# Output side of a hybrid decoder layer: projections run column block by column block, weights streamed three times, norms moved under the next block

## The chip, the cores and the metric

The kernel runs on one core of a Trainium2 chip. The metric is the device time of one execution in microseconds (us), lower is better. Engines are named as in the profile: PE is TensorE, DVE VectorE, ACT ScalarE, POOL GpSimd, SP SyncE, which here issues most transfers.

## What is computed

One layer of a decoder on 1024 prompt tokens and 64 new tokens (8 sequences of 8), all in float32. Only its second half matters here:

```
a_proj = a_out @ p['w_attn_out']          # (tokens, 512) @ (512, 1024)
b_proj = y @ p['w_ssd_out']
mixed = (gate_a * a_proj + gate_b * b_proj) @ p['w_out']   # (1024, 1024)
x = x + rmsnorm(mixed, p['post_mix_norm'])
h2 = rmsnorm(x, p['pre_ffn_norm'])
gu = h2 @ p['w_up']                       # (1024, 5632)
f = (silu(gu[..., :D_FF]) * gu[..., D_FF:]) @ p['w_down']
x = x + rmsnorm(f, p['post_ffn_norm'])
```

Ahead of it stand the input projection, a Mamba branch, the prompt attention and the attention of the new tokens over their caches (the sample stage).

## The kernel before

Tensors lie transposed: 128 channels on the partitions, T = 1088 tokens along the free axis, KD = 8 tiles of channels for a width of 1024. The tokens are cut into three column blocks c = 0, 1, 2 (`TH`: 368, 368, 352 columns), one PSUM bank each. A float32 product is made from three matmuls: every operand is split in a high part (`hH`, `aH`, `wH`) and a low part (`hL`, `aL`, `wL`), and `into` (lines 1637 to 1647) issues high by high, high by low, low by high for each tile of the inner axis (four tiles in the attention projection, eight in the output projection).

Weights come in chunks. SP loads a chunk to one of two raw buffers (`load`, line 434); POOL splits it in one of three slots (`split`: a cast, L646, and a subtraction, L648); PE multiplies with it for all three column blocks. SP may load chunk n when chunk n-2 is split, POOL may split chunk n when PE has finished with chunk n-3. Before, the attention projection has 8 chunks of 128x512 and the output projection 8 of 128x1024 elements; each serves one tile m of output channels and three blocks.

The order of each engine's work is written out by hand, and engines meet at semaphores. The stretch around the change, in its old order:

- PE: for m, for c: attention projection (bank c, freed by DVE). DVE multiplies the gates in (L1540, L1542 with the PSUM input, L1545) into `acc8`, whose start values (the Mamba branch, `ba_scr`) SP loads tile by tile together with the gates (L558, L563, L564).
- When all 24 tiles are mixed, ACT writes `hH` (L1108) and DVE `hL` (L1549); PE starts the output projection when the eight tiles of block 0 are there. ACT moves its results to `m2` (L798).
- Then the two norms, for all blocks together. ACT squares tiles of 1088 columns (L808), PE adds them up with a matrix of ones (`sums`, L1656), ACT takes the root (L816), DVE the reciprocal (L1556, L1186). DVE scales and adds to `x1` (L1559, L1562), and after the second norm writes scaled tiles and low halves (L1188, L1180).
- PE starts the feed-forward product (`up`) on block c when that block's halves are there. It has 11 groups of 4 up chunks and 2 down chunks.

SP's transfer of x (`xt_scr` to `x1`, L571) stands behind the last gates, ahead of the first chunk of `w_out`.

Of the kernel before, what the change touches and what calls it, by code (L numbers as in the profile page):

```python
# [22 lines left out]
ACT = mybir.ActivationFunctionType  # L23
# [6 lines left out]
P = 128  # L30
# [48 lines left out]
U_NORME = U_OUT + KD + 1  # L79
U_NORMF = U_NORME + 1  # L80
U_FF = U_NORMF
# [8 lines left out]
C_OUT = C_PROJ + KD  # L90
C_FF = C_OUT + KD
# [3 lines left out]
def trunk(nc, x_prompt, x_sample, cache0, cache1, cache2, state_conv, state_ssm, pre_mix_norm, w_in,  # L95
# [5 lines left out]
    with ctx:  # L101
# [56 lines left out]
        base[0] += 3 * T * 4  # L158
# [24 lines left out]
        rs = at("rs", [P, T], off=T0 + 2 * T * 4)  # L183

# [67 lines left out]
        G, A = ps[0:3], ps[3:8]  # L252
        RING = [G[0], G[1], G[2], A[0]]
# [22 lines left out]
        def gap(c, rows=P):  # L276
            return G[c][0:rows, 0:TH[c][1] - TH[c][0]]

# [28 lines left out]
        ba_in, xt_in, x1_done, facc_zero = sem("ba_in"), sem("xt_in"), sem("x1_done"), sem("facc_zero")  # L307
# [33 lines left out]
        mix_in = [sem(f"mix_in{m}") for m in range(KD)]  # L341
# [58 lines left out]
        def stages():  # L400
# [3 lines left out]
            yield C_OUT, 1, lambda i: [(wou[:, :, m * P:(m + 1) * P], KD, P) for m in range(KD)]  # L404
# [8 lines left out]
        def _(sp):  # L413
# [94 lines left out]
            for stage, (first, rounds, chunks) in enumerate(stages()):  # L508
                per = len(chunks(0))
                if stage == 2:  # L510
# [28 lines left out]
                    load_k(1)  # L539

# [7 lines left out]
                    for m in range(2):  # L548
                        load(C_PROJ + m, wao[:, :, m * P:(m + 1) * P], NJ, P, C_PROJ + m)
                    sp.wait_ge(spv_ready, DB - 1)  # L550
                    load_v(DB - 1)

                    for q in gate_out:
                        sp.wait_ge(q, 32 * KD + 1)
                    sp.wait_ge(g_ready[2], U_PROJ - 1)
                    for m in range(2):
                        for k in range(2):
                            sp.dma_start(gates[k][:, m, :], gate_scr[k, m]).then_inc(mix_in[m], 16)  # L558
                    sp.wait_ge(spv_ready, DB)
                    for m in range(KD):  # L560
                        if m >= 2:
                            for k in range(2):
                                sp.dma_start(gates[k][:, m, :], gate_scr[k, m]).then_inc(mix_in[m], 16)  # L563
                        sp.dma_start(acc8[:, m, :], ba_scr[:, m, :]).then_inc(mix_in[m], 16)  # L564
                        if m + 2 < KD:
                            load(C_PROJ + m + 2, wao[:, :, (m + 2) * P:(m + 3) * P], NJ, P, C_PROJ + m + 2)
                    continue
                if stage == 3:
                    sp.wait_ge(aL_ready, 2 * NJ + 1)

                    sp.dma_start(x1[:, :, :], xt_scr).then_inc(xt_in, 16)  # L571
# [39 lines left out]
        def _(pool):  # L611
# [158 lines left out]
            for m in range(KD):  # L770
                split(C_PROJ + m, U_PROJ + max(m - 2, -1), NJ, P, C_PROJ + m)
            for m in range(KD):
                split(C_OUT + m, U_OUT + m - 2, KD, P, C_OUT + m)
            for t in range(3):
                split(C_FF + t, U_OUT + 6 + t, KD, P, C_FF + t)
            pool.wait_ge(x1_done, 2 * KD)
# [16 lines left out]
        def _(act):  # L793
# [311 lines left out]
            act.wait_ge(mix_step, 9 * KD)  # L1105
            for c in range(3):
                for f in range(KD):
                    act.copy(cols(hH[:, f, :], c), cols(acc8[:, f, :], c)).then_inc(hH_ready, 1)  # L1108
            for m in range(KD):
                for c in range(3):  # L1110
                    evac(c, U_OUT + m + 1, [(cols(m2[:, m, :], c), gap(c))])
            for c in range(3):
                act.wait_ge(g_free[c], U_OUT + KD)
            squares(m2, KD, 8, 7)
            roots(KD, U_NORME)
            squares(x1, KD, 16, 14, lambda f: act.wait_ge(x1_done, 2 * f + 2))
            roots(KD, U_NORMF)
            halves(3 * KD)

            act.wait_ge(hL_ready, 72)  # L1120

            def hidden(k, u):
# [972 lines left out]
```

## Time and profile before

| | us |
|---|---|
| median of 3 runs | 3412.22 (3406.45 to 3413.03) |
| the profiled execution | 3417.95 |
| its span, first to last instruction | 3415.0 |
| PE busy, share of the span | 91% |
| mean granted clock of PE | 0.933 |

The profiled execution is 5.7 us longer than the median, and 2.95 us of it lie outside its span. Times inside it are given from the start of the span.

### The profile page before, as it was taken

What the parts mean: (1) busy time and instruction counts of PE and PEld (TensorE: products, weight loads), DVE (VectorE), ACT (ScalarE), POOL (GpSimd) and SP (SyncE); (2) the same over time, 40 slices, a digit from 0 to 9 for tenths busy, and PEclk for the clock granted to TensorE, in tenths of its full rate; (3) what the DMA queues carried; (4) which work ended last, traced back from release to release, by engine and by line L of the source; (5) the groups of instructions that cost most, each with busy time, mean ns of one, the idle gap of its engine ahead of it and who ended that gap; (6) DMA issues with size and microseconds to landing.
All of it is one profiled execution on the core that took longest, in us unless ns stands there. A gap on an engine that the chain in (4) does not pass through costs nothing.

```text
span 3415.0 us, 47987 instructions
## 1 busy us (share of the span) xinstructions
PE 3107.6 (91%) x18365; PEld 2886.6 (85%) x18365; DVE 1394.7 (41%) x2781; ACT 736.8 (22%) x1632; POOL 771.1 (23%) x539
## 2 busy tenths in 40 slices
PE   5699999999999999999999927998887999999998
PEld 3698898899789889989899925778867999999997
DVE  4566648556654755222122251113334223322225
ACT  3232132313312320232232211110122000000003
POOL 1222222222222122212121000001312322322222
PEclk8799999999999999999999967777999999999999
DMA  4233333424333342112212054445300111111112
GB/s 140 84 125 116 104 130 85 158 90 124 115 102 120 103 145 91 46 41 56 61 35 67 17 135 125 139 143 197 114 28 25 44 44 44 49 42 48 44 44 67
DMA packets 324378, 297.59 MB, mean 87 GB/s; under 512 B 23232, under 2 KB 291056, under 8 KB 322840
## 3 DMA queue, kind: packets, MB, share of 16 engines
q1 hardware_dynamic: 240502, 239.40, 22.8%
q10 hardware_dynamic: 83674, 55.24, 5.5%
q8 instruction: 158, 2.59, 0.3%
q14 instruction: 44, 0.36, 0.0%
HBM read 247.00 MB, written 101.34 MB: 102 GB/s over the span
## 4 chain that ended last, share of the span: by engine, by line
PE 85%; DVE 9%; DMA 2%; issue 2%; ACT 1%; SPq 1%; POOL 0%; DVEq 0%; ACTq 0%; POOLq 0%
PE ps L1644 21%; PE ps L1646 21%; PE ps L1645 21%; PE ps L1969 3%; DVE ssde L1304 2%; PE ps L1746 2%; PE ps L1849 2%; PE ps L1870 2%; PE ps L1919 1%; PE ps L1753 1%; PE ps L1752 1%; PE ps L1861 1%; PE ps L1798 1%; PE ps L1795 1%; PE ps L1656 1%
## 5 line engine op out<-in xcount | busy, mean ns | idle before, releaser
L1644 PE MATMUL ps<-hH,wH 128*128 128x368 f32 (+2 forms) x3480 | 1165.5, 335 | 55.2 <-issue 44.7
L1646 PE MATMUL ps<-hH,wL 128*128 128x368 f32 (+2 forms) x3480 | 1146.0, 329 | 0.0
L1645 PE MATMUL ps<-hL,wH 128*128 128x368 f32 (+2 forms) x3480 | 1145.5, 329 | 0.0
L1644 PEld LDWEIGHTS ps<-hH,wH 128*128 128x128 f32 (+1 forms) x3480 | 657.8, 189 | 101.2 <-issue 84.0
L1645 PEld LDWEIGHTS ps<-hL,wH 128*128 128x128 f32 (+1 forms) x3480 | 658.2, 189 | 1.9
L1646 PEld LDWEIGHTS ps<-hH,wL 128*128 128x128 f32 (+1 forms) x3480 | 657.2, 189 | 2.1
L646 POOL CAST wH<-wraw 128x1024 fp32r<-128x1024 f32 (+2 forms) x191 | 195.5, 1024 | 1787.5 <-PE ps L1646 1306.1
L648 POOL TENSOR_TENSOR wL<-wraw,wH 128x1024 fp32r<-128x1024 f32 (+2 forms) x191 | 451.4, 2363 | 15.3
L1575 DVE TENSOR_TENSOR sq<-sq,ps 128x368 f32<-128x368 f32 (+1 forms) x66 | 35.1, 532 | 434.0 <-PE ps L1646 434.0
L1446 DVE COPY atp<-ps 128x256 f32<-128x256 f32 (+1 forms) x96 | 52.5, 547 | 328.1 <-PE ps L1861 328.1
L1644 PE MATMUL ps<-uH,wH 128*128 128x368 f32 (+1 forms) x528 | 176.0, 333 | 0.7 <-DVE m L1584 0.7
L1645 PE MATMUL ps<-uL,wH 128*128 128x368 f32 (+1 forms) x528 | 173.6, 329 | 0.0
L1646 PE MATMUL ps<-uH,wL 128*128 128x368 f32 (+1 forms) x528 | 173.4, 328 | 0.0
L1584 DVE TENSOR_TENSOR m<-m,ps 128x368 f32<-128x368 f32 (+1 forms) x240 | 123.3, 530 | 81.1 <-PE ps L1646 79.8
L1644 PE MATMUL ps<-yH,wH 128*128 128x368 f32 (+1 forms) x384 | 129.5, 337 | 22.3 <-DVE gpart L1421 17.0
L1304 DVE SCALAR_TENSOR_TENSOR ssde<-ssde,tokg,ssdbcb 128x128 f32<-128x128 f32 (+1 forms) x288 | 132.1, 526 | 11.0 <-ACT ssdbcb L900 11.0
L798 ACT COPY qkv<-ps 128x368 f32<-128x368 f32 (+1 forms) x108 | 59.1, 547 | 341.6 <-PE ps L1646 288.7
L1969 PE MATMUL ps<-smpt,smvraw 128*128 128x16 f32 x576 | 115.9, 351 | 17.2 <-DMA smvn<-out_dram 10.4
L1969 PEld LDWEIGHTS ps<-smpt,smvraw 128*128 128x128 f32 x576 | 112.7, 301 | 19.4 <-issue 18.5
L1295 DVE SCALAR_TENSOR_TENSOR ssdc<-ssdc,ccg,ssdc 128x1112 f32<-128x1112 f32 x72 | 109.7, 1524 | 46.8 <-ACT ssdc L938 45.1
L1645 PE MATMUL ps<-yL,wH 128*128 128x368 f32 (+1 forms) x384 | 127.3, 332 | 0.0
L1646 PE MATMUL ps<-yH,wL 128*128 128x368 f32 (+1 forms) x384 | 127.1, 331 | 0.0
(295 smaller groups left out, 3976.7 us busy)
## 6 DMA issues: line engine op xcount, KB each, us to landing
wraw<-in_w_in_dram SPq DMA_DIRECT2D x92, 512.0 KB, 3.9
wraw<-in_w_up_dram SPq DMA_DIRECT2D x44, 512.0 KB, 3.8
ssdcr<-cum_scr ACTq DMA_DIRECT2D x32, 512.0 KB, 4.8
out_dram<-in_cache_kv_w_dram SPq DMA_DIRECT2D x16, 960.0 KB, 5.5
wraw<-in_w_down_dram SPq DMA_DIRECT2D x22, 512.0 KB, 3.7
smkraw<-in_cache_kv_w_dram SPq DMA_DIRECT2D x40, 256.0 KB, 6.6
smvraw<-in_cache_kv_w_dram SPq DMA_DIRECT2D x40, 256.0 KB
ssds<-in_state_ssm_dram ACTq DMA_DIRECT2D x16, 512.0 KB, 5.4
```

Of the source, the lines that this page charges most:

```text
L646: pool.tensor_copy(wH[b][:, 0:k], a[:, 0:k]).then_inc(w_hi, 1)
L648: pool.tensor_tensor(wL[b][:, 0:k], a[:, 0:k], wH[b][:, 0:k].bitcast(F32), ALU.subtract).then_inc(w_split, 1)
L1295: dve.scalar_tensor_tensor(out=cacc[:, 0:CWID - 3], in0=cr[:, i:i + CWID - 3], scalar=ccg[:, m, 24 + i:25 + i], in1=cacc[:, 0:CWID - 3], o ...
L1304: ins = dve.scalar_tensor_tensor(out=dec[c % 2][0:n, h, 0:n], in0=dec[c % 2][0:n, h, 0:n], scalar=tokg[0:n, c, 1, h:h + 1], in1=bcb[0:n, P ...
L1584: dve.tensor_tensor(cols(m2[:, m, :], c), cols(m2[:, m, :], c), gff(c, m + 1), ALU.add).then_inc(g_free[c], 1)
L1644: pe.matmul(dst, hi, cols(mH[:, k, :], c), start=k == 0, stop=False)
L1645: pe.matmul(dst, hi, cols(mL[:, k, :], c), start=False, stop=False)
L1646: last = pe.matmul(dst, lo, cols(mH[:, k, :], c), start=False, stop=k == kt - 1)
L1746: pe.matmul(A[2][0:n, h * 64:h * 64 + 64], dec[c % 2][0:n, h, 0:n], xtok[0:n, h * 64:h * 64 + 64], start=True, stop=True)
L1849: mm = pe.matmul(A[1 + s][:, 0:w], tokens(qT, gr, i)[rows], keys(kT, gr, i)[rows], start=True, stop=True)
L1870: mm = pe.matmul(A[4][:, 64 * s:64 * s + 64], pt[i % 2][:, s * len(bl) + b, :], vtok[gr][:, t, 64 * s:64 * s + 64], start=b == 0, stop=b = ...
L1969: pe.matmul(A[4][:, 16 * j:16 * j + 16], vraw[:, t, j * P:(j + 1) * P], pts[:, t, 16 * j:16 * j + 16], start=t == 0, stop=False)
```

## The change

- The attention projection goes block by block: for c, for m. Its chunks are now 128x1024 and hold two m; the four of them are loaded and split three times (12 instead of 8 small ones). The same holds for the output projection: 8 chunks, three times (24).
- PE writes to a ring of six banks (`RING6`) instead of one bank a block.
- DVE mixes a block at a time. The halves of block 0 are made before blocks 1 and 2 are mixed.
- ACT squares each tile of 368 columns as it evicts it, and DVE adds the squares up (`out_square`, `x1_square`), where PE did. PE issues one sum a norm and block (`e_sums`, `f_sums`). The norms of block c stand among the products of block c + 1 on all three engines; those of block 2 stand under the first feed-forward products of blocks 0 and 1, which are reordered for it.
- SP loads all gates in the sample stage, and ba_scr in three transfers, one a block.

```diff
 (SP)
+                    for m in range(KD):
+                        for k in range(2):
+                            sp.dma_start(gates[k][:, m, :], gate_scr[k, m]).then_inc(gates_in, 16)
                     with sp.Fori(0, DB - 2) as b:
...
+                    for c in range(3):
+                        sp.dma_start(cols3(acc8, c), cols3(ba_scr, c)).then_inc(ba_in[c], 16)
+                    for n in range(2, 3 * (KD // 2)):
+                        load_proj(n)
+                        if n == 5:
+                            sp.wait_ge(aL_ready, 2 * NJ + 1)
+                            sp.dma_start(x1[:, :, :], xt_scr).then_inc(xt_in, 16)
+                    for n in range(3 * KD):
+                        m = n % KD
+                        load(C_OUT + n, wou[:, :, m * P:(m + 1) * P], KD, P, C_OUT + n)
 (POOL)
+            for n in range(C_PROJ, C_FF + 3):
+                c, u = last_use(n - SPL)
+                pool.wait_ge(g_ready[c], u)
+                kt, w = (NJ, 2 * P) if n < C_OUT else (KD, P)
+                split(n, 0, kt, w, n, guard=False)
 (ACT)
+            def out_evict(c, m):
...
+                act.copy(cols(m2[:, m, :], c), src)
...
+                    if n >= 3:
+                        act.wait_ge(essum_step, (KD - 1) * c + max(m - 2, 0))
+                act.activation(dst[:, 0:w], src, ACT.Square).then_inc(g_free[c], 1)
 (DVE)
+            mix(0)
+            mixed_low(0)
+            mix(1)
+            mix(2)
+            mixed_low(1)
+            mixed_low(2)
+            for m in range(1, KD):
+                out_square(0, m)
             dve.wait_ge(xt_in, 16)
...
+            for c in range(2):
+                factor_e(c)
+                x1_rows(c, 0, 4)
+                out_square(c + 1, 1)
+                x1_rows(c, 4, 8)
+                out_square(c + 1, 2)
+                out_square(c + 1, 3)
+                factor_f(c)
+                h2_rows(c, 0, 3)
...
+            factor_e(2)
+            x1_rows(2, 0, 8)
+            factor_f(2)
+            h2_rows(2, 0, 8)
 (PE)
+            for c in range(3):
+                for m in range(KD):
+                    out_product(c, m)
+                    if c and m == 0:
+                        e_sums(c - 1)
+                    if c and m == 4:
+                        f_sums(c - 1)
...
+            pe.wait_ge(hL_ready, 48 + 2 * KD)
...
+            up_part(0, 0)
+            e_sums(2)
+            up_part(0, 1)
...
+            up_part(1, 0)
+            up_part(1, 1)
...
+            up_part(2, 0)
+            f_sums(2)
+            up_part(2, 1)
+            pe.wait_ge(hL_ready, 48 + 3 * KD)
+            for i in range(3):
+                up_part(i, 2)
```

On DVE, the norms began before as follows (after the last low half of the mixing; `rs` holds the factors of all blocks, `m_165` is m2, `x_166` x1):

```order
L1556 RECIPROCAL rs<-rs 128x368 x2
L1556 RECIPROCAL rs<-rs 128x352
L1559 SCALAR_TENSOR_TENSOR m_165<-m_165,nrm,rs 128x1088
L1562 TENSOR_TENSOR x_166<-x_166,m_165 128x1088
L1559 SCALAR_TENSOR_TENSOR m_165<-m_165,nrm,rs 128x1088
```

And this is DVE's queue now where the second norm of block 1 begins (`mid_96` collects block 2's squares of the output, `mid_92` and `mid_93` hold one tile's; `mid_97` is the factor, `mid_98` and `mid_99` scaled tiles):

```order
L1643 TENSOR_TENSOR mid_96<-mid_96,mid_93 128x352
L1683 RECIPROCAL mid_97<-mid_97 128x368
L1697 SCALAR_TENSOR_TENSOR mid_98<-x_175,nrm,mid_97 128x368
L1697 SCALAR_TENSOR_TENSOR mid_99<-x_175,nrm,mid_97 128x368
L1689 TENSOR_TENSOR hL<-mid_98,hH 128x368
L1697 SCALAR_TENSOR_TENSOR mid_98<-x_175,nrm,mid_97 128x368
L1689 TENSOR_TENSOR hL<-mid_99,hH 128x368
L1643 TENSOR_TENSOR mid_96<-mid_96,mid_92 128x352
```

The norm of one block and the square additions of the next stand in one queue, and every tile is a block wide instead of 1088 columns. The additions of 352 columns are block 2's, the rest is block 1's.

On SP, before, the transfers behind the last V rows began with the gates of tiles 0 and 1; this piece is the middle of them:

```order
L558 DMA gate_a<-gate_scr 128x1088
L558 DMA gate_b<-gate_scr 128x1088
L564 DMA acc_73<-ba_scr 128x1088
L434 DMA wraw_52<-in_w_attn_out_dram 128x4x128
L564 DMA acc_73<-ba_scr 128x1088
L434 DMA wraw_51<-in_w_attn_out_dram 128x4x128
L563 DMA gate_a<-gate_scr 128x1088
L563 DMA gate_b<-gate_scr 128x1088
```

Now:

```order
L570 DMA acc_73<-ba_scr 128x8x368 x2
L570 DMA acc_73<-ba_scr 128x8x352
L440 DMA wraw_52<-in_w_attn_out_dram 128x4x256
L440 DMA wraw_51<-in_w_attn_out_dram 128x4x256
L440 DMA wraw_52<-in_w_attn_out_dram 128x4x256
L440 DMA wraw_51<-in_w_attn_out_dram 128x4x256
L575 DMA x_175<-xt_scr 128x8704
L440 DMA wraw_52<-in_w_attn_out_dram 128x4x256
```

The gates are gone from here, all of ba_scr stands ahead of the third chunk, and the transfer of x ahead of the seventh.

## Rows read from the trace of the kernel before

**Rows 1.** The page: span; busy us, share and instructions of each engine.

```profile
span 3415.0 us, 47987 instructions
PE 3107.6 (91%) x18365; PEld 2886.6 (85%) x18365; DVE 1394.7 (41%) x2781; ACT 736.8 (22%) x1632; POOL 771.1 (23%) x539
```

**Rows 2.** Busy time by stage: stretch, its length, engines, PE's granted clock, DMA share, GB/s.

```profile
2359.00:2410.00 51.00, 49.60 (x288) 49.30 (x288) 42.57 (x71) 0.00 (x0) 15.88 (x14) 0.97 0.96 357
2410.00:2421.00 11.00, 0.21 (x1) 0.24 (x2) 10.34 (x12) 9.06 (x23) 7.86 (x5) 0.66 0.47 142
2421.00:2517.40 96.40, 96.31 (x576) 96.02 (x576) 6.79 (x16) 11.23 (x26) 24.01 (x14) 0.99 0.13 39
2517.40:2599.00 81.60, 49.42 (x170) 34.42 (x171) 57.91 (x70) 36.75 (x52) 10.74 (x3) 0.81 0.02 7
2599.00:2634.60 35.60, 35.60 (x218) 35.60 (x217) 5.68 (x7) 2.94 (x5) 10.31 (x6) 1.00 0.15 45
```

**Rows 3.** POOL in order of time, feed-forward part: start us, us.

```profile
2610.90 1.04 POOL L646 CAST wH<-wraw 128x1024 fp32r<-128x1024 f32 x1 [8.36 <-PE ps L1646]
2612.02 2.40 POOL L648 TENSOR_TENSOR wL<-wraw,wH 128x1024 fp32r<-128x1024 f32 x1
...
2622.76 1.04 POOL L646 CAST wH<-wraw 128x1024 fp32r<-128x1024 f32 x1 [8.34 <-PE ps L1646]
```

**Rows 4.** POOL in order of time, in the feed-forward loop.

```profile
2771.44 1.04 POOL L646 CAST wH<-wraw 128x1024 fp32r<-128x1024 f32 x1 [26.32 <-PE ps L1646]
...
2774.90 1.04 POOL L646 CAST wH<-wraw 128x1024 fp32r<-128x1024 f32 x1
...
2780.12 1.04 POOL L646 CAST wH<-wraw 128x1024 fp32r<-128x1024 f32 x1 [1.73 <-DMA wraw<-in_w_up_dram]
```

**Rows 5.** DMA issues, 2380 to 2420: count, KB each, us to landing.

```profile
x<-xt_scr SPq DMA_DIRECT2D x1, 4352.0 KB, 19.9
wraw<-in_w_out_dram SPq DMA_DIRECT2D x5, 512.0 KB, 3.6
```

**Rows 6.** POOL in order of time, first chunks of w_out.

```profile
2410.20 1.33 POOL L646 CAST wH<-wraw 128x1024 fp32r<-128x1024 f32 x1
2411.61 2.51 POOL L648 TENSOR_TENSOR wL<-wraw,wH 128x1024 fp32r<-128x1024 f32 x1
2414.09 1.32 POOL L646 CAST wH<-wraw 128x1024 fp32r<-128x1024 f32 x1
```

**Rows 7.** DVE in order of time, the same stretch.

```profile
2407.95 2.68 DVE L1540 TENSOR_TENSOR acc<-acc,gate_b 128x352 f32<-128x352 f32 x1
2410.55 0.51 DVE L1542 TENSOR_TENSOR gate_a<-gate_a,ps 128x352 f32<-128x352 f32 x1
...
2412.47 2.05 DVE L1549 TENSOR_TENSOR hL<-acc,hH 128x368 fp32r<-128x368 f32 x1 [0.56 <-ACT hH L1108]
```

**Rows 8.** DVE in order of time, one mixing and the next.

```profile
2376.50 0.53 DVE L1540 TENSOR_TENSOR acc<-acc,gate_b 128x368 f32<-128x368 f32 x1
...
2378.03 0.52 DVE L1540 TENSOR_TENSOR acc<-acc,gate_b 128x352 f32<-128x352 f32 x1
```

**Rows 9.** DVE in order of time, the second norm.

```profile
2564.05 2.45 DVE L1186 RECIPROCAL rs<-rs 128x368 f32<-128x368 f32 x1 [2.79 <-ACT rs L816]
...
2567.71 0.54 DVE L1180 TENSOR_TENSOR hL<-sq,hH 128x368 fp32r<-128x368 f32 x1
2568.17 0.59 DVE L1188 SCALAR_TENSOR_TENSOR sq<-x,nrm,rs 128x368 f32<-128x368 f32 x1
2568.68 0.53 DVE L1180 TENSOR_TENSOR hL<-sq,hH 128x368 fp32r<-128x368 f32 x1
```

**Rows 10.** DVE's first mixing and what it waited for.

```profile
2361.86 0.54 DVE L1540 TENSOR_TENSOR acc<-acc,gate_b 128x368 f32<-128x368 f32 x1 [2.80 <-DMA acc<-ba_scr]
```

**Rows 11.** PE in order of time, sample stage: transposes of the third batch's K rows.

```profile
2121.82 0.90 PE L1919 MATMUL ps<-ident,smkraw 128*128 128x128 f32 x3
```

**Rows 12.** ACT in order of time: roots of the first norm.

```profile
2531.47 1.28 ACT L816 ACT_TABLE_LOAD   x1
2532.79 1.76 ACT L816 ACTIVATE rs<-ps,eps 128x368 f32<-128x368 f32 x3
```

More of the change, by code:

```diff
@@ L183, in trunk @@
         rs = at("rs", [P, T], off=T0 + 2 * T * 4)
+        sE1, sqE0, sqE1, sqF0, sqF1, sE0, sF, hv0, hv1 = [at(f"mid{i}", [P, TH[0][1]], off=T0 + i * TH[0][1] * 4) for i in range(9)]
+        sE, sqE, sqF, hvb = [sE0, sE1], [sqE0, sqE1], [sqF0, sqF1], [hv0, hv1]
         xs = at("xs", [P, XT, T], off=X1)
@@ L1109, in _ @@
             for m in range(KD):
[L1110 to L1122, printed above, removed]
+                out_evict(0, m)
@@ new lines, in silu_first @@
+            def silu_first(c):
+                act.wait_ge(g_ready[c], U_FF + 1)
+                act.activation(cols(sq[0], c), gff(c, 1), ACT.Silu).then_inc(g_free[c], 1)
+            root_e(2)
+            act.wait_ge(uL_ready, 1)
+            for f in range(0, 4):
+                x1_square(2, f)
+            silu_first(0)
+            for f in range(4, 8):
+                x1_square(2, f)
+            silu_first(1)
+            root_f(2)
+            for f in range(8):
+                h2_high(2, f)
@@ L1124, in hidden @@
+            silu_first(2)
+            def hidden(k, u, first=False):
                 par = k_par(k)
                 for i in range(2):
-                    for c in range(3):
+                    for c in (() if first and i == 0 else range(3)):
                         act.wait_ge(uL_ready, k * 2 + i + 1)
@@ L1139, in k_par @@
                 return 1 if k_even[0] else 0
[L1141 removed]
+            hidden(0, U_FF, first=True)
             with act.Fori(0, 5) as i:
@@ L1996, in _ @@
-            sums(KD, U_NORME, 8)
-            sums(KD, U_NORMF, 16)
-            def up(n, u, n0, first=False):
+            for c in range(3):
+                pe.wait_ge(g_free[c], U_PROJ)
+            for c in range(3):
+                for m in range(KD):
+                    n, k = c * KD + m, C_PROJ + c * (KD // 2) + m // 2
+                    if m % 2 == 0:
+                        pe.wait_ge(w_split, k + 2)
+                    if n >= 6:
+                        cp, mp = LAST[n - 6]
+                        pe.wait_ge(g_free[cp], U_PROJ + mp + 1)
+                    into(RING6[n % 6][:, 0:TH[c][1] - TH[c][0]], c, k % SPL, NJ, 2 * P, m % 2 * P, P, aH, aL)
@@ new lines, in out_product, with e_sums @@
+            def out_product(c, m):
+                n, k = c * KD + m, C_OUT + c * KD + m
+                pe.wait_ge(w_split, k + 2)
+                if m == 0:
+                    pe.wait_ge(hL_ready, 24 + KD * (c + 1))
+                cp, mp = LAST[n - 6]
+                pe.wait_ge(g_free[cp], (U_OUT if n >= 6 else U_PROJ) + mp + 1)
+                into(RING6[n % 6][:, 0:TH[c][1] - TH[c][0]], c, k % SPL, KD, P, 0, P, hH, hL)
+            def e_sums(c):
+                w = TH[c][1] - TH[c][0]
+                pe.wait_ge(essum_step, (KD - 1) * (c + 1))
+                if c:
+                    pe.wait_ge(rsE_act, c)
+                pe.matmul(A[3][:, 0:w], ones[:, :], sE[c % 2][:, 0:w], start=True, stop=True).then_inc(esum_ready, 1)
@@ new lines, in f_sums @@
+            def f_sums(c):
+                w = TH[c][1] - TH[c][0]
+                pe.wait_ge(fssum_step, (KD - 1) * (c + 1))
+                if c:
+                    pe.wait_ge(rsF_act, c)
+                pe.matmul(A[4][:, 0:w], ones[:, :], sF[:, 0:w], start=True, stop=True).then_inc(fsum_ready, 1)
+            for c in range(3):
+                for m in range(KD):
+                    out_product(c, m)
[3 more added lines that the diff above has]
+                        f_sums(c - 1)
```

238 lines of the change are left out of this document (166 added, 72 removed).

## The prediction

> **What bounds the kernel now.** The page gives the whole: a span of 3415.0 us in a run of 3417.95 us, TensorE busy for 91% of it, no other engine above 41% [rows 1]. Shares do not price this change, so the next view is the busy time by stage: one row each for projection, gap, output projection, norms and the first four chunks of the feed-forward product [rows 2]. I call that stretch, 2359.0 to 2634.6, the middle: 275.6 us. The reader is to see where TensorE is not full: 11 us between projection and output projection (0.21 us busy), and 81.6 us behind the output projection with 170 recorded matmuls.
>
> What must be done there on TensorE is 288 + 576 + 288 = 1152 matmuls. In the feed-forward part four splits of GpSimd in a row, of which two are shown, each released by TensorE's last matmul on an older chunk, follow one another every 11.86 us [rows 3], and a chunk is 3 blocks of 24 matmuls: 0.165 us per matmul, 3.95 us per block. So 1152 matmuls are 190 us, and 86 us of the middle are waits, sums of squares and half clock. That is all the change can win, 2.5%. The half clock is in the windows too: the mean granted clock is 0.97 over the 51 us of the projection, which starts after a wait, and 1.00 in the feed-forward part. If it was at the lower level (1.2 for 2.4 GHz) for 3 us, 1.5 us were lost; I take 1.6 us for each start after a wait of some 10 us.
>
> **What the change removes.** The 11 us go (mixing of all 24 tiles, then their halves), since the halves of block 0 are ready early. Of the norms, blocks 0 and 1 go under products; only block 2 stays in the open, under five of its neighbours' products. If nothing else were late, the middle would be 190 + 4 (six sums) plus what is left open, priced with the rivals.
>
> **What it adds.** 1. Weights. 12 + 24 chunks instead of 8 small + 8: each chunk now feeds 24 matmuls, 3.95 us, not 11.86 us. A split of 1024 columns is 1.04 + 2.40 us and repeats after 3.46 us when GpSimd is alone [rows 3, 4]. A load lands 3.6 us after its issue [rows 5], just about the length of one split, and two raw buffers take turns. GpSimd alone would hold TensorE's pace by 0.5 us a chunk.
>
> 2. The port. GpSimd is not alone. In [rows 6] and [rows 7] both engines are saturated for a moment. A VectorE operation with both inputs in SBUF takes 0.53 us [rows 8], but 2.68 and 2.05 us when it meets GpSimd's subtraction, and GpSimd's cast stretches from 1.04 to 1.33 us. One cycle of cast and subtraction is then 3.89 us and lets through just two such VectorE operations at 0.4 us of work: the split itself holds the other off for 3.1 us. The multiplication that reads PSUM (L1542) keeps its 0.51 us beside GpSimd. A reciprocal (2.4 us, one SBUF input) stands beside a split in no row; the nearest is L1542, also with one SBUF input, so I let the six run free. Held, each waits at most one subtraction more, 6 x 2.2 = 13 us. [...]
>
> Before, the middle had 12 full-size splits, most of them far apart. Now it has 38 of them: 38 x 3.1 = 118 us. VectorE's operations with two SBUF inputs are 48 (mixing), 24 (low halves), 21 + 21 (sums of squares, which TensorE did before), 24 additions, 24 low halves of the second norm: 162 at 0.45 us from start to start, and 48 scalings at 0.51, 97 us [rows 9]. Together 215 us on one lock, against 190 us of TensorE. So I take VectorE with GpSimd as the new bound, and follow their chain.
>
> 3. The start. ba_scr now comes in three transfers of a block, 1472 KB instead of 544 KB for the first. At the 357 GB/s of this stage [rows 2] that is 2.7 us more, so the first mixing starts at 2364.5 instead of 2361.86 [rows 10]. The third weight chunk queues behind all three blocks (12.5 us), so TensorE, done with two chunks at 2368, waits some 9 us. x1 (4352 KB) takes 10 to 20 us in the queue [rows 5] and holds the seventh chunk for some 5 us. Both waits lie ahead of a VectorE that is late anyway.
>
> 4. The gates (16 x 544 KB, 8.9 MB) move into the sample stage, behind the K rows of the second batch. At 357 GB/s they run to about 2113 and the next K rows, queued behind them, land by 2121; the transposes that need them start at 2121.8 [rows 11]. Zero on the path, with 1 us to spare.
>
> **The chain, from the first mixing.**
> - To the first sum e(0), a sum standing behind block 0's seven square additions: VectorE's 24 mixings at 1.53 us [rows 8], 24 halves and 7 additions at 0.45 are 50.7 us; 22 splits (chunks 3 to 24) are 68.2 us; the 24 multiplications that run beside them take off 10.8. 2364.5 + 108.1 = 2472.6.
> - e(0) to f(0): sum 0.6, table 1.28, root 0.6, reciprocal 2.4 [rows 9, 12]; 8 scalings, 8 additions, 7 square additions and one of the next block are 11.3; TensorE makes four products meanwhile, so four splits, 12.4. Together 28.6: 2501.2. TensorE's four products need 15.8, so it waits about 10 us at f(0).
> - f(0) to e(1): 3.6 + 20 operations 9.5 + four splits 12.4 = 25.5: 2526.7.
> - e(1) to f(1): 27.3 (no table): 2554.0. f(1) to the last halves of block 1: 3.6 + 9.5 + three splits 9.3 = 22.4: 2576.4.
> - Only then may the first feed-forward product start (it needs those halves, and the banks): 3.95 + 1.6 of half clock: 2582. Then e(2), and four products, 15.8 + 0.6 (VectorE's 14.5 fits below): 2598.4. f(2), with a table load since Silu came between, is 4.9 to the factor; eight pairs at 0.96 [rows 9] and a tail are 8.3: 2611.6. Three products of block 2 and 1.6 of half clock, 13.4, then chunk 4, 11.9: 2636.9.
>
> That is +2.3 us against 2634.6. The sum leaves out the handovers: each half norm passes some ten times between ScalarE, VectorE and TensorE at 0.05 to 0.1 us, and may begin with a split half done. 1 to 1.5 us for each of the five halves adds 6 us. The middle ends 8.6 us later. On this execution's 3417.95 that is 3427; against the median, 5.7 lower, **3421 us**.
>
> **The rivals.**
> - *VectorE keeps up* (TensorE stays the bound). For it: [rows 6, 7] hold only two cycles, and VectorE may slip in more operations where GpSimd waits for its load. Then: 190 + 4, start waits 8 + 6, block 2's norm behind f(2), 13.2 less one product, 9.3, and four restarts at half clock, 6.4: 224 us, -52, 3360 us. With half the contention, -22, 3390. It decides if the lock costs less than about 60 of the 118 us. Against it: every such pair that meets in [rows 6, 7] blocks. Chance 0.3 for both.
> - *No change, within 7 us*: the same chain without the handovers, 3414.5. 0.17.
> - *The loads starve too* (slower than forecast): behind the subtraction that frees a raw buffer, the next cast on it began 5.1 us later in the loop [rows 4] (2780.12, the other buffer's cast having begun as that subtraction ended, at 2774.90); two chunks then take 3.5 + 5.1, 4.3 us each, 0.35 too much on 36 chunks, 13 us. Or the gates run a quarter slower than 357 GB/s and the K rows come 8 us late. 3430 to 3440. 0.15.
> - *The forecast*: 0.38.
>
> **How the numbers follow.** This kernel's runs tell 0.2%, 7 us, from nothing. Faster: 0.3 and 0.03 from the low edge of the forecast's spread, 0.33. Same: 0.17 and 0.04 from that spread, 0.21. Slower: the rest, 0.46. Range: to some -50 us on one side, which leaves out the full case of "keeps up" (half of its 0.3), and to +30 on the other, where loads or held reciprocals come on top: 3367 to 3442. The forecast's own range is 3405 to 3438.
>
> **What would show it.** VectorE's two-input operations in the middle at a mean of 1 us or more, in 2.6 us steps; GpSimd's cast at 1.3 us; TensorE waiting about 10 us before each of e(1), f(0), f(1) and before the first feed-forward product; four or five falls of the granted clock. Wrong if these operations keep 0.6 us and the waits before the sums are under 3 us; or if the sample stage has grown, which would be the gates.

## The result and the profile after

The changed kernel takes 3426.76 us (median of five runs, 3424.88 to 3427.74), the kernel before 3410.95 us (five runs, 3406.45 to 3413.03). The ratio is 1.0047, 95% interval 1.0033 to 1.0062: slower by half a per cent, 15.8 us by the medians. The page of the changed kernel, span and the busy time of each engine:

```profile
span 3425.2 us, 48068 instructions
PE 3087.9 (90%) x18281; PEld 2877.5 (84%) x18281; DVE 1499.6 (44%) x2855; ACT 742.8 (22%) x1666; POOL 865.7 (25%) x579
```

Beside [rows 1], POOL has 95 us more to do and DVE 105 us; the span is 10.2 us longer, not 15.8. The missing 5.6 us are a property of the profiled executions. The last small reciprocal of the sample stage is one instruction in both programs, with the same work ahead of it but for the gates' transfers. In order of time on DVE it stands here, first in the kernel before, then in the changed kernel, then in a second profile of the kernel before (the run e9_before_again):

```profile
2315.09 0.15 DVE L1506 RECIPROCAL small<-small 64x1 f32<-64x1 f32 x1 [1.43 <-ACT sms L1087]
```

```profile
2310.47 0.15 DVE L1590 RECIPROCAL small<-small 64x1 f32<-64x1 f32 x1 [1.44 <-ACT sms L1102]
```

```profile
2308.77 0.15 DVE L1506 RECIPROCAL small<-small 64x1 f32<-64x1 f32 x1 [1.43 <-ACT sms L1087]
```

The span of that second profile is 3408.1 us. From the reciprocal to the end it is 3415.0 - 2315.1 = 1099.9 us and 3408.1 - 2308.8 = 1099.3 us in the two profiles of the kernel before, and 3425.2 - 2310.5 = 1114.7 us in the changed kernel: +14.8 us, close to what the medians say. I call this time **the tail**. For the unchanged kernel it came out the same twice, and the 6.3 us that vary lie ahead of it. The gates' transfers are priced by a run of their own (e4_gates_early).

Where the 14.8 us are, by stretches of the changed kernel (length, then busy time of PE, PEld, DVE, ACT, POOL, PE's granted clock, DMA share, GB/s): the projection, the start of the output projection, the rest up to the first sum e(0), from e(0) to the first up product, and from there to GpSimd's first split behind the middle:

```profile
2356.00:2410.00 54.00, 38.89 (x197) 38.27 (x198) 35.89 (x49) 6.49 (x13) 28.91 (x16) 0.81 0.70 253
2410.00:2424.00 14.00, 11.22 (x69) 10.63 (x67) 13.73 (x11) 1.50 (x3) 13.07 (x8) 1.00 0.37 113
2424.00:2477.00 53.00, 40.53 (x241) 39.97 (x241) 51.30 (x46) 10.65 (x25) 40.59 (x22) 0.92 0.40 119
2477.00:2584.00 107.00, 69.80 (x368) 66.43 (x368) 98.81 (x95) 30.49 (x69) 59.62 (x30) 0.80 0.25 74
2584.00:2644.50 60.50, 52.75 (x295) 52.05 (x296) 29.80 (x50) 16.34 (x28) 18.23 (x8) 0.91 0.09 27
```

The middle is now 288.4 us (2356.06 to 2644.48) for 275.5 before (2359.12 to 2634.62): +12.9. TensorE is full in none of the five, and DVE is busy for 51.3 of 53 and 98.8 of 107 us. TensorE's waits from 2300 to 2720: what it waited for, total us, times and longest:

```profile
PE ps L2186 <- DVE mid L1678: 19.3, 2, 10.3
PE ps L2179 <- DVE mid L1643: 18.9, 2, 10.6
PE ps L1812 <- POOL wL L656: 15.1, 2, 9.8
...
PE ps L1812 <- ACT mid L1136: 9.7, 1, 9.7
PE ps L1812 <- DVE hL L1689: 7.6, 1, 7.6
PE ps L1812 <- DVE gate_a L1627: 4.7, 3, 2.2
```

L2179 and L2186 are the sums of squares of a block, e for the first norm and f for the second: four waits, 38 us. e(0) is the first norm's sum of block 0. VectorE is busy so long because its operations wait inside themselves. Some of its groups from 2350 to 2700, with count, busy time and mean ns of one:

```profile
L1625 DVE TENSOR_TENSOR acc<-acc,gate_b 128x368 f32<-128x368 f32 (+1 forms) x24 | 43.4, 1809 | 6.8 <-DMA acc<-ba_scr 6.8
L1635 DVE TENSOR_TENSOR hL<-acc,hH 128x368 fp32r<-128x368 f32 (+1 forms) x24 | 28.2, 1249 | 0.0
...
L1627 DVE TENSOR_TENSOR gate_a<-gate_a,ps 128x368 f32<-128x368 f32 (+1 forms) x24 | 12.5, 521 | 10.2 <-PE ps L1814 10.1
```

L1625 reads two SBUF tiles and means 1.81 us, where one alone takes 0.53 [rows 8]. L1627, of the same size, reads one of them from PSUM and stays at 0.52. The pattern of [rows 6, 7], seen in two cycles before, now fills the stretch. First VectorE, then GpSimd, in order of time:

```profile
2396.91 2.68 DVE L1625 TENSOR_TENSOR acc<-acc,gate_b 128x368 f32<-128x368 f32 x1
2399.51 0.52 DVE L1627 TENSOR_TENSOR gate_a<-gate_a,ps 128x368 f32<-128x368 f32 x1
2400.12 0.76 DVE L1630 TENSOR_TENSOR acc<-acc,gate_a 128x368 f32<-128x368 f32 x1
2400.80 2.71 DVE L1625 TENSOR_TENSOR acc<-acc,gate_b 128x368 f32<-128x368 f32 x1
```

```profile
2396.67 2.52 POOL L656 TENSOR_TENSOR wL<-wraw,wH 128x1024 fp32r<-128x1024 f32 x1
2399.13 1.35 POOL L654 CAST wH<-wraw 128x1024 fp32r<-128x1024 f32 x1
2400.56 2.54 POOL L656 TENSOR_TENSOR wL<-wraw,wH 128x1024 fp32r<-128x1024 f32 x1
```

The operation that begins at 2396.91, during the subtraction, ends at 2399.59, 0.4 us behind the subtraction's end at 2399.19. I call this a lock: one of the two engines holds it and the other stands. Here one cycle of 3.9 us lets through one mixing of one tile.

### The profile page after: what moved, and what is told of

It is laid out like the page before. It is cut to its first block, busy times and chain, and to the rows that moved or that the text cites. A ratio compares the mean times of both kernels' runs of the same rounds, so it can differ in the third digit from the quotient of the medians.

```text
span 3425.2 us, 48068 instructions
## 1 busy us (share of the span) xinstructions
PE 3087.9 (90%) x18281; PEld 2877.5 (84%) x18281; DVE 1499.6 (44%) x2855; ACT 742.8 (22%) x1666; POOL 865.7 (25%) x579
## 4 chain that ended last, share of the span: by engine, by line
PE 81%; DVE 13%; issue 2%; DMA 2%; ACT 1%; SPq 1%; POOL 0%; DVEq 0%; ACTq 0%; POOLq 0%
PE ps L1812 20%; PE ps L1814 19%; PE ps L1813 19%; PE ps L2137 3%; DVE ssde L1388 2%; PE ps L1914 2%; PE ps L2017 2%; PE ps L2038 2%; PE ps L2087 1%; DVE acc L1625 1%; PE ps L1920 1%; PE ps L1921 1%; PE ps L2029 1%; PE ps L1966 1%; PE ps L1963 1%
## 5 line engine op out<-in xcount | busy, mean ns | idle before, releaser
L654 POOL CAST wH<-wraw 128x1024 fp32r<-128x1024 f32 (+1 forms) x211 | 230.1, 1091 | 1719.1 <-PE ps L1814 1306.0
L656 POOL TENSOR_TENSOR wL<-wraw,wH 128x1024 fp32r<-128x1024 f32 (+1 forms) x211 | 511.9, 2426 | 16.9
L813 ACT COPY qkv<-ps 128x368 f32<-128x368 f32 (+1 forms) x108 | 59.2, 548 | 341.7 <-PE ps L1814 288.8
L2137 PE MATMUL ps<-smpt,smvraw 128*128 128x16 f32 x576 | 116.5, 352 | 17.0 <-DMA smvn<-out_dram 10.1
L2137 PEld LDWEIGHTS ps<-smpt,smvraw 128*128 128x128 f32 x576 | 113.3, 302 | 19.2 <-issue 18.3
L1524 DVE CUSTOM_DVE_ANT_0 ats<-ps,atmask 128x128 f32<-128x128 f32 (+1 forms) x192 | 60.0, 350 | 155.9 <-PE ps L2017 155.9
```

The costliest lines, as they stand in the source:

```text
L654: pool.tensor_copy(wH[b][:, 0:k], a[:, 0:k]).then_inc(w_hi, 1)
L656: pool.tensor_tensor(wL[b][:, 0:k], a[:, 0:k], wH[b][:, 0:k].bitcast(F32), ALU.subtract).then_inc(w_split, 1)
L2137: pe.matmul(A[4][:, 16 * j:16 * j + 16], vraw[:, t, j * P:(j + 1) * P], pts[:, t, 16 * j:16 * j + 16], start=t == 0, stop=False)
```

## The experiments

The ratios below are to the kernel before, timed on the same chip each time. "The tail" is measured in the profile of the run, as above, and may be held against 1099.9 (before) and 1114.7 (changed). Only the kernel before has two profiles, each other kernel has one, and the tail holds two pieces that no edit touches and that still differ. So this table cuts it in three: from the reciprocal to the projection's first matmul (start), from there to GpSimd's split behind the fourth up chunk (middle), and the rest.

| kernel | start | middle | rest |
|---|---|---|---|
| before | 44.0 | 275.5 | 780.4 |
| before, second profile (e9_before_again) | 43.4 | 276.0 | 779.9 |
| e4_gates_early | 43.1 | 275.9 | 779.4 |
| changed | 45.6 | 288.4 | 780.7 |
| e1b_pool_writes | 45.4 | 233.1 | 781.0 |
| e2_small_loads | 42.8 | 289.6 | 781.7 |
| e7_one_input | 42.7 | 288.8 | 779.0 |
| e5_loads_between | 43.3 | 284.9 | 778.7 |
| e3_proj_once | 42.7 | 268.1 | 776.2 |
| e6_split_once | 44.7 | 237.2 | 774.4 |
| e8_blocks_split_once | 43.8 | 250.8 | 780.3 |
| e10_late_up_splits | 42.8 | 231.1 | 774.6 |

The start scatters by 2.9 us. The middle of the kernel before, with the gates moved or not, repeats within 0.5 us. The rest is 774.4 to 776.2 us in the three kernels with the projection once and 778.7 to 781.7 us in the others. The DMA queue of kind "instruction", from 2700 to 3200, moved this (packets, MB, share), first in the kernel before, then in e6_split_once:

```profile
q8 instruction: 31, 0.51, 0.4%
```

```profile
q8 instruction: 1, 0.02, 0.0%
```

In those three kernels it moved 1 to 3 packets there, in the other nine 30 to 33; and only the nine have waits of TensorE marked "issue" from 2645 to 3330, 2.0 to 3.4 us. The loading of instructions thus goes with the shorter rest; that it is the cause was not tested. A price of the lock is read from the middle.

**GpSimd reads nothing.** On the changed kernel.

```diff
-                split(n, 0, kt, w, n, guard=False)
+                pool.wait_ge(raw_in[n % RAW], raw_count(n, n))
+                alone(pool)
+                pool.memset(wH[n % SPL][:, :].bitcast(F32), 0.03125).then_inc(w_hi, 1)
+                pool.wait_ge(w_hi, n + 1)
...
+                pool.memset(wL[n % SPL][:, :].bitcast(F32), 0.0009765625).then_inc(w_split, 1)
```

> The changed kernel, but GpSimd's 39 splits from the first projection chunk to the third up chunk are replaced by four memsets each, one after the other, of about the same length together, which read nothing from SBUF (the weights of this stretch are constants; the loads, waits and counts stay). The lock theory: VectorE's two-input operations fall back to their price without contention (0.45 to 0.55 us for 0.8 to 1.25 us in the changed kernel), TensorE waits only for its start, for the third chunk (9.8 us) and for x1, and the middle is 40 to 55 us shorter: 3370 to 3385. The rival that the weight stream (loads, the number of chunks, the handovers GpSimd to TensorE) holds TensorE: all of that stays, so 3420 to 3430. A second rival, that the chain of handovers between ScalarE, VectorE and TensorE is by itself too long: less than half of the gain, 3400 to 3415, with waits of 5 us or more left ahead of the norms' sums.

Measured: 3369.36 us, ratio 0.9869 (0.9852 to 0.9885); tail 3367.7 - 2308.2 = 1059.5 us. GpSimd was as busy as with splits (four memsets of 0.95 us, 3.8 us a chunk), and VectorE's groups fell to their price alone. One line of POOL's memsets from 2300 to 2700, then two of VectorE's groups from 2350 to 2700:

```profile
L794 POOL MEMSET wL<- 128x1024 f32 x78 | 74.4, 954 | 4.5
```

```profile
L1631 DVE TENSOR_TENSOR acc<-acc,gate_b 128x368 f32<-128x368 f32 (+1 forms) x24 | 12.7, 530 | 6.7 <-DMA acc<-ba_scr 6.7
L1641 DVE TENSOR_TENSOR hL<-acc,hH 128x368 fp32r<-128x368 f32 (+1 forms) x24 | 10.9, 532 | 0.0
```

1809 ns became 530 and 1249 became 532. TensorE's waits for the sums e and f are gone from its list; five for POOL (18.3 us, the third chunk's 10.1 among them) and the one for the last halves (7.7) are left. The gain is 55.3 us of the middle and 57 by the medians, just past the theory's 40 to 55, and it rules out the handovers and the weight stream as the limit. It is also what "VectorE keeps up" would have been: I gave 3360. The Trainium skill, "SBUF — State Buffer", Who interferes with whom, lets a VectorE instruction with two SBUF inputs lose only against a GpSimd instruction that reads SBUF: a write-only memset takes nothing from it, and the run agrees, 0.53 us beside memsets of 0.95 us.

**Small loads.** Changed kernel, the loads of w_out cut to an eighth.

> The changed kernel, but each of the 24 loads of w_out brings one eighth of the chunk (the rest of the buffer keeps old data, and GpSimd splits the whole buffer as before). Lock theory: a load was landed in time or GpSimd was late because of VectorE; -3 to 0 us against the changed kernel, 3423 to 3427. The rival that the loads starve as well (two raw buffers, 3.6 us from issue to landing): -10 us or more, 3405 to 3417.

```diff
-                        load(C_OUT + n, wou[:, :, m * P:(m + 1) * P], KD, P, C_OUT + n)
+                        load(C_OUT + n, wou[:, 0:1, m * P:(m + 1) * P], 1, P, C_OUT + n)
```

Measured: 3425.57 us, ratio 1.0036 (1.0024 to 1.0048), tail 1114.1. A load now lands 1.9 us behind its issue and not 4.1, the middle is 1.2 us longer, and no group of TensorE's waits moves by more than 1.8 us. The loads of w_out don't starve the middle. (Those of w_attn_out do hold it up: GpSimd's third chunk is late behind ba_scr.)

**Which operations wait.** Changed kernel, the 42 square additions with one input.

> The changed kernel with the 42 additions of squares replaced by a multiplication by one with a single SBUF input, of the same output (the sums of squares are left out; the rest stays). If the lock asks for a second SBUF input, these 42 keep 0.45 us or less beside the splits (0.75 to 0.81 us in the changed kernel) and take up to 42 x 0.45 = 19 us off the lock, of which I expect 8 to 16 us on the path: 3411 to 3419. If a VectorE operation of any kind meets the lock, they stay at 0.75 us or more and the time within 3 us of the changed kernel.

```diff
-                dve.tensor_tensor(sE[c % 2][:, 0:w], sE[c % 2][:, 0:w], sqE[m % 2][:, 0:w], ALU.add).then_inc(essum_step, 1)
+                dve.tensor_scalar(sE[c % 2][:, 0:w], sqE[m % 2][:, 0:w], 1.0, None, ALU.add).then_inc(essum_step, 1)
```

(The same edit stands in the second sum.) The text on record says a multiplication by one; the edit adds one, which is the same work. Measured: 3422.01 us, ratio 1.0035 (1.0023 to 1.0047), tail 1110.5: 4 us less than the changed kernel, but the middle is 288.8 us, the same. The 8 to 16 us did not come. My premise, that only a second SBUF input takes the lock, was wrong. In order of time, VectorE, then GpSimd:

```profile
2492.99 2.49 DVE L1678 TENSOR_SCALAR mid<-mid 128x368 f32<-128x368 f32 x1
...
2496.37 0.34 DVE L1678 TENSOR_SCALAR mid<-mid 128x368 f32<-128x368 f32 x1
```

```profile
2492.76 2.52 POOL L656 TENSOR_TENSOR wL<-wraw,wH 128x1024 fp32r<-128x1024 f32 x1
```

Alone the one-input operation takes 0.34 us, less than the 0.53 of a two-input one of that size, and beside the subtraction it waits all the same. So one SBUF input does not free an operation when it runs in this faster way. The Trainium skill, "SBUF — State Buffer", Who interferes with whom, names the fast modes on two ports beside the two inputs as takers of the lock; this row agrees, if the 0.34 us are such a mode.

The shorter operations did help at first: the first up product starts 223.9 us behind the projection's first matmul, 228.0 in the changed kernel. Then the edit made a new loss. In block 2's norm one addition met GpSimd's clearing of `m2`, again VectorE, then GpSimd:

```profile
2594.69 7.18 DVE L1678 TENSOR_SCALAR mid<-mid 128x352 f32<-128x352 f32 x1 [0.31 <-ACT mid L1149]
```

```profile
2594.18 7.49 POOL L792 MEMSET m<- 128x8704 f32 x1 [22.38 <-DVE x L1660]
```

It ended 0.2 us behind the memset, and TensorE waited 4.0 us for f(2), a wait that the changed kernel does not have. There the last two additions, with two inputs each, took 1.18 us together from 2603.32 and ran on beside the same memset, begun at 2603.46. So an operation of this fast kind waits even for a GpSimd operation that only writes, and one with two inputs does not. The experiment isolates nothing; that two inputs in SBUF are the cause for the rest stands on L1627 (0.52 us with PSUM) and on the run with memsets.

**The late third chunk.** Changed kernel, weight loads between the block transfers.

> The changed kernel with the loads of the third and fourth projection chunk put between the three block transfers of ba_scr, not behind all of them. TensorE's wait of 9.8 us for the third chunk goes. The prediction said of this wait that it lies ahead of a VectorE that is late anyway: then 3423 to 3428, 0 to -3 us. The rival, that a delay of TensorE at the start runs through to the end: -8 us, 3417 to 3420.

```diff
-                    for c in range(3):
-                        sp.dma_start(cols3(acc8, c), cols3(ba_scr, c)).then_inc(ba_in[c], 16)
                     for n in range(2, 3 * (KD // 2)):
+                        if n < 5:
+                            c = n - 2
+                            sp.dma_start(cols3(acc8, c), cols3(ba_scr, c)).then_inc(ba_in[c], 16)
                         load_proj(n)
```

Measured: 3417.2 us, ratio 1.0021 (1.0012 to 1.0030), tail 3422.0 - 2315.1 = 1106.9, 7.8 us less than the changed kernel. Of these, 3.5 lie in the middle, 2.3 in the start and 2.0 in the rest, which the edit does not touch. The wait does run through, in the middle with less than the rival's 8 us. (The ratios of the two kernels are 9 us apart, with intervals that leave 1 to 17.) VectorE's waits from 2340 to 2482, changed kernel first, then this one:

```profile
DVE gate_a L1627 <- PE ps L1814: 10.1, 1, 10.1
DVE acc L1625 <- DMA acc<-ba_scr: 6.8, 1, 6.8
```

```profile
DVE acc L1626 <- DMA acc<-ba_scr: 6.7, 1, 6.7
```

In the changed kernel VectorE itself stood still for 10.1 us, until the projection's fifth product existed. With the loads between the transfers it never waits for TensorE there, and e(0) comes 115.9 us behind the projection's first matmul, not 120.8: 4.9 of the 10 us come back. By the end of the middle it is 3.5.

**One half of the change undone.** Projection once, over eight small chunks.

> The changed kernel with one of its two halves undone: the attention projection runs once over its eight small chunks, all three blocks on each, as before the change, with the mixing in that order; the output projection by column block with its weights three times, and the norms under it, stay. Lock theory: four small splits' worth less data to split before the first sum (8 x 512 instead of 12 x 1024 columns, about 8 splits of 3.1 us = 25 us less on the lock), while the gap between the projections comes back for block 0 alone (8 to 10 us). The first sum e(0) comes about 20 us sooner than the 2476.9 of the changed kernel, the rest is unchanged: 3403 to 3411. Rival, that the loss sits in the norms' chain behind e(0) and the projection is harmless: within 5 us of the changed kernel, or slower by the returned gap of 8 to 10 us (3425 to 3437).

```diff
-            for c in range(3):
-                for m in range(KD):
-                    n, k = c * KD + m, C_PROJ + c * (KD // 2) + m // 2
...
+            for m in range(KD):
+                pe.wait_ge(w_split, C_PROJ + m + 2)
+                for c in range(3):
...
+                    into(RING6[n % 6][:, 0:TH[c][1] - TH[c][0]], c, (C_PROJ + m) % SPL, NJ, P, 0, P, aH, aL)
```

The mixing follows in the same order, and ba_scr comes in three groups of feature tiles. Measured: 3398.21 us, ratio 0.9956 (0.9942 to 0.9969), tail 1087.0: 28 us less than the changed kernel, more than the 16 to 24 I wrote. Of the 28, 20.3 lie in the middle, inside what I wrote. The middle is 7.4 us shorter than before the change. The gap between the projections is back (11.2 us), yet the reciprocal behind e(0) begins 101.7 us behind the projection's first matmul, and 123.1 us in the changed kernel. The waits before f(0), e(1) and f(1) stay at 8.7 to 10.6 us. So the streaming of w_attn_out costs more than the whole change loses.

**The gates alone.** The kernel before, its gates' transfers moved.

> The kernel before with only the gates' 16 transfers moved to the sample stage, behind the K rows of the second batch. By the prediction this costs nothing there and mixing may start as early as before: within 3 us of the kernel before, 3408 to 3414. Rival, that the 8.9 MB delay the K rows: 5 to 10 us slower, 3416 to 3421. A third: the transfers ahead of the mixing being gone from the projection's stretch, up to 3 us faster, as the changed kernel's first matmul of the projection came 3.0 us earlier than before the change.

```diff
+                    for m in range(KD):
+                        for k in range(2):
+                            sp.dma_start(gates[k][:, m, :], gate_scr[k, m]).then_inc(mix_in[m], 16)
...
-                        if m >= 2:
-                            for k in range(2):
-                                sp.dma_start(gates[k][:, m, :], gate_scr[k, m]).then_inc(mix_in[m], 16)
```

Measured: 3409.78 us, ratio 0.9992 (0.9983 to 1.0001), tail 1098.4, middle 275.9. No price.

**w_out split once.** On e3_proj_once, with the halves kept.

> The kernel with the projection once, and the eight chunks of w_out split once: their halves are written to DRAM (1 MB a chunk) and blocks 1 and 2 load them ready, so GpSimd splits nothing between the first sum e(0) and the up chunks; products, norms and their order stay. Lock theory: from e(0) on VectorE has some 30 us of work for two half norms against 31.6 us of TensorE, so the waits of 8 to 10 us ahead of f(0), e(1), f(1) fall to 0 to 3 us, and the 16 splits take 35 to 45 us with them: 3353 to 3368, faster than the kernel before. Rival, the 20 MB more in transfers, or 1 MB loads that land late for a product of 3.95 us: waits of TensorE for the halves instead, 3380 to 3400. Rival, the handovers are the limit: 3385 to 3398.

```diff
+                    def store_split(m):
+                        sp.wait_ge(w_split, C_OUT + m + 2)
+                        sp.dma_start(wou_scr[m], wHL[:, :, (C_OUT + m) % SPL, :].bitcast(F32)).then_inc(ba_in[m % SPL], 16)
...
+                    for i in range(KD, 3 * KD):
+                        n = C_OUT + i
...
+                        sp.dma_start(wHL[:, :, n % SPL, :].bitcast(F32), wou_scr[i % KD]).then_inc(raw_in[n % RAW], 16)
```

GpSimd only passes the count on for these sixteen. Measured: 3368.97 us, ratio 0.9878 (0.9862 to 0.9893), 41 us less than the kernel before and 1 us above the range I had given it; tail 1056.3, middle 237.2. From e(0) to the last output product TensorE is full (the stretch, columns as above):

```profile
2450.00:2514.00 64.00, 63.56 (x376) 62.30 (x375) 54.07 (x87) 27.56 (x63) 5.70 (x4) 0.99 0.70 235
```

The DMA engines are 70% busy and 1 MB lands in 5.2 us, in time but for the first of them: ahead of it TensorE waits 3.4 us (5.4 in e8_blocks_split_once), a small piece of the rival. One wait of 9.9 us follows, for ScalarE's eviction of the last output products, which stands behind VectorE's last halves of block 1. VectorE there, then GpSimd:

```profile
2509.86 2.61 DVE L1723 SCALAR_TENSOR_TENSOR mid<-x,nrm,mid 128x368 f32<-128x368 f32 x1
2512.40 1.37 DVE L1715 TENSOR_TENSOR hL<-mid,hH 128x368 fp32r<-128x368 f32 x1
2513.81 2.56 DVE L1723 SCALAR_TENSOR_TENSOR mid<-x,nrm,mid 128x368 f32<-128x368 f32 x1
```

```profile
2509.51 2.57 POOL L672 TENSOR_TENSOR wHL<-wraw,wHL 128x1024 fp32r<-128x1024 f32 x1
2512.02 1.35 POOL L670 CAST wHL<-wraw 128x1024 fp32r<-128x1024 f32 x1
2513.45 2.52 POOL L672 TENSOR_TENSOR wHL<-wraw,wHL 128x1024 fp32r<-128x1024 f32 x1
```

It is the lock again, with the splits of the first up chunks.

**The same with the projection by column block.**

> The changed kernel with both column-block loops kept (attention projection too, with its 12 chunks of 1024 columns split as before), and w_out split once, its halves kept in DRAM and loaded ready for blocks 1 and 2. Up to the first sum e(0) only two of 22 splits fall away, so e(0) stays within 6 us of the changed kernel (166 us behind the last reciprocal of the attention stage, against 168.7); behind it TensorE's waits of 8 to 10 us ahead of f(0), e(1) and f(1) go, as they went in the kernel with the projection once. Lock theory: 25 to 35 us faster than the changed kernel, 3390 to 3402, and 20 to 33 us slower than the kernel with the projection once. Rival, that the projection by column block costs nothing by itself: within 8 us of 3369.

The edit is that of e6_split_once, on the changed kernel. Measured: 3386.76 us, ratio 0.9929 (0.9915 to 0.9942), tail 3385.0 - 2310.2 = 1074.8. Behind e(0) 35 us are gone (from its reciprocal to the end 3385.0 - 2474.0 = 911.0 us, and 3425.2 - 2479.2 = 946.0 in the changed kernel); ahead of it, in the middle, 3.1. The distance to e6_split_once is 18 us by the medians and 13.6 in the middle: the price of the projection by column block, its twelve large splits with the late third chunk, less the gap that is gone. That is under the 20 to 33 I wrote, as the total is a little under my 3390.

**Up chunks later.** On e6_split_once.

> The kernel that splits w_out once, with one more wait: GpSimd starts the split of the second up chunk only when the low halves of block 1 are ready. In the profile TensorE waits 9.9 us ahead of the first up product, while VectorE finishes these halves beside three splits of up chunks. With two of the three splits out of the way this wait falls by about 5 us; the two splits now lie beside the second norm half of block 2, where they may cost 2 to 5 us, or be late for the product that needs them (4 us behind the first). Lock theory: -5 to +1 us against 3369. Rival, that the splits are now late: +3 to +8 us.

```diff
                 pool.wait_ge(g_ready[c], u)
+                if n == C_FF + 1:
+                    pool.wait_ge(hL_ready, 48 + 2 * KD)
```

Measured: 3363.5 us, ratio 0.9861 (0.9846 to 0.9876), tail 3361.9 - 2313.4 = 1048.5. The wait fell from 9.9 to 4.1 us and the middle from 237.2 to 231.1. The total is 5.5 us under 3369, just past the 5 I wrote. This is the fastest kernel here that leaves nothing out, 1.4% under the kernel before. Its interval overlaps that of e6_split_once; the middle (6.0 us apart) and the wait (5.8) tell the two apart, in one profile each.

**The kernel before once more.**

> The kernel before, unchanged, profiled once more. The stretch up to the last reciprocal of the attention stage came out at 2303 to 2315 us in the profiles of this case, and the rest of a run agreed with its median: the kernel before 1099.9 us from there to its end, the changed kernel 1114.7 (+14.8 us, for +15.8 of the medians). If the first part is what varies from run to run, the second profile of the kernel before shows 1098 to 1102 us behind that reciprocal whatever its total; if not, it differs by more than 4 us there.

Measured: 3409.88 us in one run, tail 1099.3, inside the 1098 to 1102 I wrote. For this kernel only the part ahead of the tail moved. That part is 2303.0 to 2315.5 us long over the profiles of all these kernels. Between kernels the tail's start and rest differ too, as the table shows.

## Why the prediction was right, and where it was off

The forecast was 3421 us, 8.8 above the kernel before as known then; the changed kernel takes 3426.76, 15.8 above it. That the time lies in the stated range says little: the range was 75 us wide, and "slower" had 0.46. What speaks for the mechanism are the places and sizes of the waits.

**The mechanism** held: VectorE and GpSimd on one lock are the bound of the middle. VectorE's 210 operations with two SBUF inputs mean 1.00 us (207.9 us busy in all), just the sign's 1 us. GpSimd's cast takes 1.35 us where the two meet, and TensorE waits 9.0, 8.3 and 10.3 us before f(0), e(1) and f(1) and 9.7 before the first up product: all named. The 10.6 us ahead of e(0) were not. The edit with memsets takes the waits before all these sums away; keeping the halves does so too, but for the 9.9 us ahead of the first up product, where splits remain. One more sign was off: the granted clock fell not four or five times but behind eight waits of 5.3 to 10.6 us (0.50, the level of 1.2 GHz, from 2476.9 to 2481.0, for instance). Most of these lie where VectorE is late anyway.

**The sum** was 8.6 us, the middle lost 12.9. By steps, forecast and measured (sums by their first matmul):

| step | forecast | measured |
|---|---|---|
| start of projection to first mixing | 5.4 | 6.7 |
| first mixing to e(0) | 108.1 | 114.1 |
| e(0) to f(0) | 28.6 | 28.4 |
| f(0) to e(1) | 25.5 | 27.0 |
| e(1) to f(1) | 27.3 | 28.4 |
| f(1) to the first up product | 22.4 | 23.5 |
| from there to the end | 60.5 | 60.4 |

The five steps behind e(0) sum to 164.3 and came out at 167.6: 3.3 us more, of the 6 that I had added there for handovers in five halves. The step that failed is the one to e(0), 7.3 us too short. The two errors have opposite signs, so the total looks better than its parts.

The sentence that failed is "Both waits lie ahead of a VectorE that is late anyway". The waits of TensorE had the right size (9.8 us for some 9, and 5.3 for some 5); that the first costs nothing was wrong. The chain counted 50.7 us of VectorE and 68.2 us of splits as if one of the two always held the lock. But VectorE used up the products there were by 2369.5 and then stood still for 10.1 us, waiting for TensorE, which waited for GpSimd's third chunk. Two splits (at 2372.13 and 2375.53) ran in that time and so did not hold VectorE up, 2 x 3.1 us: 10.1 - 6.2 leaves 3.9 of the 6.0 us that the step from the first mixing is too short. The other 2.1 us spread over the twenty splits left, at 3.2 us each and not 3.1, with 0.4 us of waiting for ScalarE in it. e5_loads_between moves two loads, the wait goes, and e(0) comes 4.9 us sooner, near the 3.9; the subtraction of the two splits itself was read, not tested.

**A count** was off as well: the middle has 40 full-size splits, not 38, and had 14, not 12. The chain by steps has the right 37 up to the last halves of block 1. And the last row of [rows 2] holds three of the four up chunks (218 of 288 matmuls); the first lies in the row of the norms.

**The place of the loss.** I had put the middle's price on splits as such. The runs divide it. Undone alone, the repeated projection weights give back 20.3 us of the middle (e3_proj_once), the repeated splits of w_out 37.7 (e8_blocks_split_once), both together 51.3 (e6_split_once, 237.2). Against these 51.3 stands what is left of the change, the output projection by column block with its norms below it: 275.5 - 237.2 = 38.4 us. The difference is the 12.9 us of the middle.

**The profiled time.** I took 5.7 us off, since the profiled run of before lay that far above the median. The two tails of before, 1099.9 and 1099.3, confirm that this offset lies ahead of the middle. Of the 14.8 us of the tail, 12.9 are the middle. The start gives 1.6 more, inside its scatter of 2.9, and the rest 0.3.

**The edits costed at nothing** were so: the gates (e4_gates_early), the loads of w_out (e2_small_loads). That the six reciprocals run free beside a split is left open: in the changed kernel no split ran beside them. One, begun at 2607.90 beside the memset of `m2`, took 2.35 us, as the one of that size at 2591.20 did alone.

**The rivals.** "VectorE keeps up" was refused by the lock at full price; its 3360 is near what the kernel does once the lock is free (3369.36 with memsets, 3363.5 in e10_late_up_splits). "No change" was the chain without its handovers, +2.3 us; it fails by the wait ahead of e(0) more than by the handovers. "The loads starve too" is refused for w_out by e2_small_loads and for the gates by e4_gates_early, though the time lies halfway between the forecast's 3421 and its 3430.

## What to carry to other kernels

Before weights are streamed again, count what they cost on the engine that prepares them, and on whom that engine holds up: here an extra split of 3.5 us on an engine that is idle for three quarters of the span took some 3.1 us from another. If prepared data are used more than once, keep the prepared form and let the DMA engines bring it again, here busy for less than a third of the span (28% before the change). And a sum of two engines on one lock is a bound only while one of them always has work; look first for the stretch in which one waits for a third. When two traces are compared, cut them where the edit ends: here 4 to 6 us of some gains lay in a loop that no edit touched.

## What the runs showed of the hardware

The turn on the lock is not always one by one. In the changed kernel, behind e(0), VectorE was in the middle of a row of two-input operations without a pause when GpSimd's cast began at 2484.31. Five more of VectorE's began after that and passed first, the last of them at 2486.43; then VectorE's next was the one to wait. VectorE's last two rows, then GpSimd's:

```profile
2486.43 0.53 DVE L1643 TENSOR_TENSOR mid<-mid,mid 128x368 f32<-128x368 f32 x1
2486.89 4.03 DVE L1654 SCALAR_TENSOR_TENSOR m<-m,nrm,mid 128x368 f32<-128x368 f32 x2
```

```profile
2484.31 3.56 POOL L654 CAST wH<-wraw 128x1024 fp32r<-128x1024 f32 x1 [13.24 <-PE ps L1814]
2487.94 2.57 POOL L656 TENSOR_TENSOR wL<-wraw,wH 128x1024 fp32r<-128x1024 f32 x1
```

The cast takes 1.04 us alone and took 3.56 here. In the cycles shown further above, only two of VectorE's operations came between two subtractions. What decides it was not tested.
